# Decay mask moved into a matmul, per-head subtraction in one instruction, state scaling moved to GpSimd, and one set of row exponentials made a group earlier

## The reference, cut to what matters

```python
a_cs = jnp.cumsum((dt * a)...)                       # decay exponents, summed inside a chunk
seg = a_cs[..., :, None] - a_cs[..., None, :]        # row exponent minus column exponent
decay = jnp.exp(jnp.where(causal, seg, -jnp.inf))    # masked: zero above the diagonal
cb = jnp.einsum('bclgn,bcsgn->bcgls', cm, bm)
y_diag = jnp.einsum('bcgls,bcgjls,bcsgjp->bclgjp', cb, decay, xdt)
def step(s, inp):
    dec, st = inp
    return dec[..., None, None] * s + st, s          # the state from chunk to chunk
y_off = jnp.einsum('bclgn,bcgjpn,bcgjl->bclgjp', cm, s_prev, jnp.exp(a_cs))
```

## Time and profile before

| | |
|---|---|
| median of 3 runs | 1851.03 us |
| profiled execution, its own time | 1850.61 us |
| its span | 1849.0 us |
| TensorE busy / VectorE / ScalarE / GpSimd | 88% / 39% / 22% / 14% of the span |
| mean granted TensorE clock | 0.957 of full |
| the SSD groups, from the first group's last x transposes | 134.05 us to 692.44 us of the span |

### The profile page before, as it was taken

One profiled execution on the slowest core, in us unless ns is written; L12 is line 12 of the kernel. 1 busy time (PEld: TensorE's weight loads), 2 busy tenths in 40 slices (PEclk: granted clock), 3 DMA queues, 4 the chain that ended last, 5 costly groups with the idle time before them and its releaser, 6 DMA issues. The chain is left out here.

```text
span 1849.0 us, 23337 instructions
## 1 busy us (share of the span) xinstructions
PE 1635.9 (88%) x9042; PEld 872.5 (47%) x9043; DVE 729.7 (39%) x1304; ACT 413.0 (22%) x769; POOL 264.6 (14%) x287
## 2 busy tenths in 40 slices
PE   4998798799789769999999999999999958999893
PEld 2554454354445334544545545444656434555451
DVE  2545644664654564700016766214025122222124
ACT  4332323233233232000013332410110111111112
POOL 0004402412330440000000000000000012222122
PEclk9998999899899989999999999999989969999997
DMA  9710101011021016712111100214340656998994
GB/s 348 293 46 1 46 23 46 32 37 46 1 91 46 1 49 244 253 46 93 46 46 45 46 18 28 91 46 153 138 181 1 227 224 231 393 343 290 393 385 155
DMA packets 106755, 241.24 MB, mean 130 GB/s; under 512 B 5481, under 2 KB 15214, under 8 KB 106690
## 3 DMA queue, kind: packets, MB, share of 16 engines
q1 hardware_dynamic: 86800, 180.60, 27.1%
q0 software_dynamic: 14288, 48.96, 7.4%
q10 hardware_dynamic: 5602, 10.78, 1.6%
HBM read 218.31 MB, written 22.02 MB: 130 GB/s over the span
## 5 line engine op out<-in xcount | busy, mean ns | idle before, releaser
L439 PE MATMUL psum<-arena 128*128 128x512 f32 x688 | 302.8, 596 | 10.6 <-ACT arena L1279 4.4
L439 PEld LDWEIGHTS psum<-arena 128*128 128x128 f32 x688 | 128.6, 190 | 168.2 <-issue 160.9
L1075 PE MATMUL psum<-arena 128*32 128x256 f32 x2816 | 165.5, 387 | 1.6 <-DVE arena L2193 1.5
L453 PE MATMUL psum<-arena 128*128 128x512 f32 x352 | 155.4, 601 | 1.6 <-issue 1.6
L627 PE MATMUL psum<-arena 128*128 128x512 f32 x256 | 124.9, 626 | 1.0 <-ACT arena L1319 1.0
L1075 PEld LDWEIGHTS psum<-arena 128*32 128x32 f32 x2816 | 91.9, 111 | 60.0 <-issue 7.0
L764 PE MATMUL psum<-arena 128*128 128x512 f32 x256 | 111.5, 593 | 0.0
L453 PEld LDWEIGHTS psum<-arena 128*128 128x128 f32 x352 | 67.3, 193 | 84.0 <-issue 83.7
L2301 POOL TENSOR_TENSOR arena<-arena 128x512 f32<-128x512 f32 x64 | 84.2, 1327 | 131.9 <-ACT arena L1374 131.9
L1729 DVE SCALAR_TENSOR_TENSOR arena<-arena 128x772 f32<-128x772 f32 (+1 forms) x96 | 93.9, 978 | 3.4
L2271 POOL TENSOR_TENSOR arena<-arena 128x512 f32<-128x512 f32 x40 | 46.5, 1174 | 336.1 <-ACT arena L1319 282.1
(11 more groups left out here) (363 smaller groups left out, 2122.8 us busy)
## 6 DMA issues: line engine op xcount, KB each, us to landing
arena<-exp_w_d SPq DMA_DIRECT2D x48, 2048.0 KB, 17.3
arena<-w_in_d SPq DMA_DIRECT2D x22, 2048.0 KB, 7.9
arena<-ada_w_d POOLq DMA_DIRECT2D x8, 2048.0 KB, 9.3
slots<-arena POOLq DMA_DIRECT2D x1, 9216.0 KB, 27.1
arena<-ada_w_d SPq DMA_DIRECT2D x4, 2048.0 KB, 21.5
arena<-ssd_proj_d SPq DMA_DIRECT2D x4, 2048.0 KB, 9.8
slots<-arena POOLq DMA_DIRECT2D x92, 64.0 KB, 4.9
arena<-slots POOLq DMA_DIRECT2D x22, 256.0 KB, 6.0
```

What stands on the lines that cost most here:

```text
L439: ins = mmul(ps[:, 0:T], slot[:, k, m * P:(m + 1) * P], src[:, k, C:NT], start=(k == 0), stop=(k == KD - 1))
L453: ins = mmul(ps[:, 0:n], src[:, k, t * P:(t + 1) * P], slot[:, k, 0:n], start=(k == 0), stop=(k == KD - 1))
L1075: ins = mmul(psU[q * R:(q + 1) * R, 0:2 * HF], XT[:, k % 2, k // 2, :], w13[p][:, :, k, q * HF:(q + 1) * HF], start=(k == 0), stop=(k == K ...
```

## The change

- `rows_of` gets a second matmul, `identb` times `shut[d]`, added into the same bank. `shut[d]` is a bf16 square, 0 where the mask is 1 and -1e30 where it is 0. It lies in memory of `tmpd[0]` and is made once.
- `exponents` is one `tensor_tensor` over 512 columns without the clamp. `cb` is one unmasked copy, and GpSimd multiplies both directions by it.
- GpSimd scales the states (`scale_state`) into a new tile `Send`; VectorE waits for it and adds kv.
- E of direction 0 of group g+1 is made during the direction-1 decays of group g (`spread(g + 1, 0, b)` after each pair). Group 0 makes its own as before.
- `Z_FRONT` is 10 and not 11, two steps of z stand ahead of `first_state`, and the middle one of `Z_STATES` is 2 and not 3.
- `add_square` comes after all `finish` calls of a group. Two small constants (`d_col`, the epsilon) are made at the start.

```diff
-        Z_FRONT = 11
-        Z_STATES = (3, 3, 3, 2, 2)
+        Z_FRONT = 10
+        Z_STATES = (3, 3, 2, 2, 2)
...
                     pe.wait_ge(*is_free(("acsT", d)))
-                    ins = mmul(ps[:, :], selb[0:3 * SH, hh:hh + 1].to_broadcast([3 * SH, P]),
-                               rowsT[0:3 * SH, d, :], start=True, stop=True)
+                    mmul(ps[:, :], selb[0:3 * SH, hh:hh + 1].to_broadcast([3 * SH, P]),
+                         rowsT[0:3 * SH, d, :], start=True, stop=False)
+                    ins = mmul(ps[:, :].rearrange("p (c l) -> p c l", c=TL), identb,
+                               shut[d].unsqueeze(1).to_broadcast([P, TL, P]), start=False, stop=True)
...
+                z_part(2)
                 first_state(0, 4, 8)
                 for i in range(2, 6):
                     for b in range(2):
-                        spread((i - 2) // 2, (i - 2) % 2 * 2 + b)
+                        if g == 0 or i >= 4:
+                            spread(g, (i - 2) // 2, (i - 2) % 2 * 2 + b)
...
                             for i in range(2 * b + 2, min(2 * b + 4, 7)):
                                 next_part(g + 1, i)
+                            if g < SG - 1:
+                                spread(g + 1, 0, b)
... ScalarE
                         run(mm[n % NM], mm[n % NM], ACT.Exp).then_inc(S_("decay_ready"), 1)
+                        if d and g < SG - 1 and h in (3, 5, 7):
+                            spread_out(g + 1, 0, (h - 3) // 2)
                     if d == 0:
                         z_silu(3)
+                if g < SG - 1:
+                    spread_out(g + 1, 0, 3)
... VectorE
-                            step(v.tensor_tensor(heads(vtmp), heads(S[(i - 1) % 2]), per_head(eend), ALU.mult))
-                            ins = v.tensor_tensor(S[i % 2], vtmp, bank(key)[:, :], ALU.add)
+                            dve.wait_ge(S_("S_scaled"), (g * 2 + d) * 3 + i - 1)
+                            ins = v.tensor_tensor(S[i % 2], Send, bank(key)[:, :], ALU.add)
...
-                    for c in range(TL):
-                        ins = v.tensor_scalar(mm[n % NM][:, c, :], bank(key)[:, c * P:(c + 1) * P],
-                                              acs[:, TC + c, at:at + 1], 0.0, ALU.subtract, ALU.min)
-                    ins.then_inc(is_free(key)[0], 1)
+                    v.tensor_tensor(mm[n % NM], bank(key)[:, :].rearrange("p (c l) -> p c l", c=TL),
+                                    acs[:, TC:TT, at:at + 1].to_broadcast([P, TL, P]), ALU.subtract).then_inc(is_free(key)[0], 1)
...
-                    if b:
-                        add_square(g, b - 1)
...
                 finish(2)
                 finish(3)
+                for b in range(3):
+                    add_square(g, b)
... GpSimd
+                def scale_state(d, i):
+                    pool.wait_ge(*is_free(("kv", g, d, i - 1)))
+                    hs = d * SH + g * HPG
+                    g_.tensor_tensor(heads(Send), heads(S[(i - 1) % 2]),
+                                     eend[:, ORDER[d][i], hs:hs + HPG].unsqueeze(2).to_broadcast([P, HPG, SHD]),
+                                     ALU.mult).then_inc(S_("S_scaled"), 1)
...
                 for i in range(2, 5):
                     make_xw(0, i)
+                    scale_state(0, i)
...
-                        g_.tensor_tensor(mm[n % NM], mm[n % NM], cb[d], ALU.mult).then_inc(S_("M_ready"), 1)
+                        g_.tensor_tensor(mm[n % NM], mm[n % NM], cb, ALU.mult).then_inc(S_("M_ready"), 1)
                         if d == 0 and h in (1, 2, 4):
                             make_xw(1, 2 + h // 2)
+                        if d == 0 and h in (1, 3, 4):
+                            scale_state(1, 2 + h // 2)
```

More of the change, by code:

```diff
@@ L175, in build @@
         cb_mem = top[0]
-        cb = [alloc(TL, P) for _ in range(2)]
+        cb = alloc(TL, P)
         NM = 4
@@ L179, in build @@
         S = [alloc(GW) for _ in range(2)]
+        Send = alloc(GW)
         assert top[0] - cb_mem >= KD * 512 and tok_mem + KD * 512 <= top[0]
@@ L192, in build @@
         d_col = small[:, 0:SI // P]
+        shut = [tmpd[0].rearrange("p t h -> p (t h)")[:, 0:P].bitcast(BF16)[:, d * P:(d + 1) * P] for d in range(2)]
         assert RAW % 2 == 0
@@ L641, in rows_of, with spread @@
                     pe.wait_ge(*is_free(("acsT", d)))
-                    ins = mmul(ps[:, :], selb[0:3 * SH, hh:hh + 1].to_broadcast([3 * SH, P]),
-                               rowsT[0:3 * SH, d, :], start=True, stop=True)
+                    mmul(ps[:, :], selb[0:3 * SH, hh:hh + 1].to_broadcast([3 * SH, P]),
+                         rowsT[0:3 * SH, d, :], start=True, stop=False)
+                    ins = mmul(ps[:, :].rearrange("p (c l) -> p c l", c=TL), identb,
+                               shut[d].unsqueeze(1).to_broadcast([P, TL, P]), start=False, stop=True)
                     ins.then_inc(is_full(key)[0], 1)
-                def spread(d, b):
+                def spread(g, d, b):
                     key = ("E", g, d, b)
@@ L1321, in xtok_evac @@
                     blk = g * 4 + m
-                    if blk == 0:
-                        act.wait_ge(S_("d_cols"), 1)
                     run(yT[:, blk, :], yT[:, blk, :], ACT.Identity, scale=d_col[:, blk:blk + 1], bias=0.0)\
@@ L1361, in _, with spread_out @@
                 xtok_evac(3)
-                for d in range(2):
+                def spread_out(g, d, b):
+                    key = ("E", g, d, b)
+                    act.wait_ge(*is_full(key))
+                    run(E[d][:, b, :], bank(key)[:, :], ACT.Exp).then_inc(is_free(key)[0], 1)
+                if g == 0:
                     for b in range(HPG // 2):
-                        key = ("E", g, d, b)
-                        act.wait_ge(*is_full(key))
-                        run(E[d][:, b, :], bank(key)[:, :], ACT.Exp).then_inc(is_free(key)[0], 1)
+                        spread_out(0, 0, b)
                 for d in range(2):
@@ L1369, in _ @@
                         z_silu(1)
+                        for b in range(HPG // 2):
+                            spread_out(g, 1, b)
                         z_silu(2)
@@ L1391, in _ @@
             act.wait_ge(*is_full(("rrow",)))
-            act.wait_ge(S_("eps_set"), 1)
             run(rrow, bank(("rrow",))[:, :], ACT.Sqrt, scale=1.0 / SI, bias=small[:, 62:63]).then_inc(is_free(("rrow",))[0], 1)
@@ L1680, in _ @@
                     .then_inc(S_("hT_ready"), 1)
+            dve.wait_ge(S_("rows_in"), 16)
+            step(v.memset(small[:, 62:63], EPS))
+            step(v.tensor_copy(d_col[0:SHD, :], r_("ssd_d")[0:SHD, 0::2]))
+            step(v.tensor_copy(d_col[SHD:P, :], r_("ssd_d")[SHD:P, 1::2]))
             for i in range(2):
@@ L1689, in _ @@
             dve.wait_ge(S_("rows_in"), 16)
-            v.tensor_copy(d_col[0:SHD, :], r_("ssd_d")[0:SHD, 0::2])
-            v.tensor_copy(d_col[SHD:P, :], r_("ssd_d")[SHD:P, 1::2]).then_inc(S_("d_cols"), 1)
             dve.wait_ge(*is_full(("dt",)))
@@ L1747, in _ @@
             dve.wait_ge(S_("consts_in"), 16 * 2)
+            for d in range(2):
+                v.tensor_scalar(shut[d], mask[d], -1.0, 1e30, ALU.add, ALU.mult)
             step(v.tensor_copy(identb, ident))
@@ L1790, in _ @@
                     dve.wait_ge(S_("M_ready"), g * 2 * HPG)
[L1791 to L1795, removed]
-                ins.then_inc(is_free(key)[0], 1)
+                v.tensor_copy(cb, bank(key)[:, :].rearrange("p (c l) -> p c l", c=TL)).then_inc(is_free(key)[0], 1)
                 conv(g, "x", 2)
@@ L1882, in _ @@
                 finish(3)
+                for b in range(3):
+                    add_square(g, b)
             add_square(SG - 1, 3)
             dve.sem_inc(S_("ssum_ready"), 1)
-            v.memset(small[:, 62:63], EPS).then_inc(S_("eps_set"), 1)
             for s in range(4, 12):
```

## The result

| | before | after |
|---|---|---|
| median (runs) | 1851.78 us (4) | 1810.12 us (4; 1807.78 to 1811.38) |
| ratio, 95% interval | | 0.9774 (0.976 to 0.9788) |
| profiled execution, its own time | 1850.61 us | 1807.78 us |
| its span | 1849.0 us | 1806.2 us |
| VectorE / GpSimd busy in the span | 729.7 / 264.6 us | 665.0 / 282.8 us |

The forecast was 1814 us. The time lies 4 us from it and well inside the range. The sum behind it was less exact than that: -36.8 us were forecast, and the two profiled executions differ by 42.8. A, D0 and D1 gained 11.3 us more than forecast; the second group's projections and the code ahead of the first A lost 5.7 us that the forecast did not have. That these partly hide each other is luck: without those 5.7 us the time would lie 9 to 10 us from the forecast and not 4. And experiment 1 shows that one term (A) was right for a reason that is half wrong.

A forecast was written before the change was run, and what follows sets the result against it. TensorE, busy 88% of the span, was taken as the bound: its work, waits and clock. Terms -28.1 - 11.2 + 5.2 - 2.7 = -36.8 us took 1850.61 to 1813.8, stated as 1814 us, range 1798 to 1836.

The forecast's parts named there:

- A: Stretch from the last x transposes to the first rows (states of direction 0): 23.3 us, -28.1 us over four groups.
- D0: Stretch from the first rows to the last product of direction 0: 31.9 us a group, -11.2 us over four groups.
- D1: Rest of the group after direction 0's last product: +1.6 us in three groups, +0.4 in the last, +5.2 in all.
- (a): In A: transposes 0.89 us sooner, two z steps fill 1.78 of 2.27 us waiting for xw; 0.5 us stays.
- (b): In A: early E removes the 2.68 us wait ahead of the second off in groups 1 to 3; group 0 keeps 0.6.
- (c): In A: GpSimd's scaling (1.04 us, up to 1.49) is hidden; xdt queued behind costs the fourth state about 0.3 us.
- rival 1: Shorter waits keep the clock at 2.4 GHz, in D0 and behind each last pair: 11.6 us, giving 1802; chance 0.15.
- rival 2: Mask matmuls at 0.38 us add 10, L1816 at 1.62 in three steps of each A another 4: 1828; chance 0.22.
- The last wait of D0: Ahead of direction 0's last pair: 5.4 us left of the 6.76 us chain, of which TensorE still waits 4.5.
- Group ends: Moving add_square finishes y and the B and C copies 1.3 us earlier, cutting two TensorE waits: -2.7 us.
- Rival 3: In D0, direction 1's scalings queue behind products on GpSimd: 10.1 us a group, 40.6 in all, 1854; chance 0.07.
- Rival 4: Waits only move: A gives about 14 us, the masks take 14, so 1850, no change; chance 0.06.

The follow-up runs named there:

- experiment 1: Changed kernel with the early E undone, every group making its own E of direction 0: 1808.63 us, ratio 0.9758.
- Experiment 3: Changed kernel with the subtraction as four instructions again, with the clamp, mask matmul kept: 1821.49 us, ratio 0.9835.
- experiment 10: Changed kernel with add_square between the finish calls again: 1817.41 us, ratio 0.98.
- experiment 6: Changed kernel with ScalarE's squares of y's first three blocks ahead of the Exp of the next group's last E: 1805.12 us, ratio 0.9753.
- experiment 5: Changed kernel with VectorE's subtraction for direction 0's head 7 ahead of direction 1's last state step: 1786.86 us, ratio 0.9658.

## Why the prediction was right, point by point

- **Stretch A: right in sum, the reason half wrong.** 23.3 us was forecast, 22.74 measured; (a) left a wait of 0.4 us (forecast 0.5), and the first group's wait ahead of the second off is 0.56 (forecast 0.6). Point (b) gave the gain at the second off in groups 1 to 3 to the early E. The first group, which has no early E, should have told me otherwise: by my own sum its wait fell from 2.7 to 0.6 through the scaling alone. Experiment 1 shows that the same holds in every group. What the early E saves in A (2.3 us a group) it costs in D1 and in ScalarE's order. (c) was too careful: no step of A waits for xdt. The terms written down add up to 23.0 us and not 23.3; without the 0.3 of (c) they give 22.7, which is what was measured.
- **Stretch D0: the step that was mis-sized.** The walk head by head gave pairs at 8.4, 15.0, 22.4 and 30.75 us; they came at 8.3, 15.0, 21.9 and 30.18. I then left a low clock of 1.2 us a group in. It was not there: the clock of the four D0 was 1.00, 0.97, 1.00 and 0.97, and the 0.97 cost nothing, as all four took 30.18 us. So of the 6.9 us that D0 gained beyond the forecast 4.6 are the clock and 2.3 the walk. The *old* D0 had a clock of 0.84 to 0.90. This is the first half of rival 1, and it held; the second half (full clock behind the last pair) did not, as the wait there stayed. Experiment 3 has 1.5 to 1.6 us for a fall of the clock in D0, in three groups of four.
- **The mask matmuls: right.** 0.22 us each in place. Doubled they cost 0.09 each on the average (0.16 to 0.18 in D0, less in D1), and rival 2 (0.38 each) falls. Its other 4 us do not follow from its own terms either: an addition of 1.62 and not 0.69 us is 0.93 more, within the slack of 1.1.
- **The rule against GpSimd, and the port.** Each scaling took 1.04 us, 1.5 times VectorE's 0.69, in line with the row the forecast used and less than the "about twice" of the Trainium skill ("GPSIMD Engine Reference", "Engine selection"). What counts is that it stands beside off and L1827. VectorE's additions to y, which were to meet GpSimd more often, met it less: the median of 32 was 0.72 us and the longest 1.81, against 1.37 and 1.68 before.
- **The last wait of D0: right.** 5.38 us of chain, 4.33 of wait, low clock behind it. (By the rows of before TensorE works 6.76 - 5.70 = 1.06 us of the chain, so the forecast's own 5.4 gives 4.3 and not 4.5.)
- **D1: too dear.** The last pair came 21.7 us after D1's first row, as walked (21.75). The stretch as a whole grew by less than forecast in the first and third group (+0.6 and +0.4, clock 0.94 against 0.90 before) and by more in the second (+2.4, 0.91 against 0.94). In the last group it fell by 1.7, of which 1.3 are the wait for `finish` (2.1 to 0.8), as forecast.
- **Group ends: one step failed.** "Y is finished 1.3 us earlier after the last pair, and so are ScalarE's copies of B and C": the first half holds (experiment 10). The second does not, because the last of the new Exps stands in ScalarE's queue ahead of all four squares. Before, the squares of y's first two blocks were taken ahead of the last pair; now all four wait for TensorE's last spread, which starts 0.9 us behind that pair, and the copy comes 6.4 us behind the pair and not 5.1. So the wait grew by 1.3 us where I had it shrink by 1.3. I had moved the four spreads past TensorE's and ScalarE's bank waits, but not past ScalarE's squares. Experiments 1 and 6 both undo it, to 3.3 and 3.9 us.
- **Rival 3** (scalings behind products) did not come: the scaling is nowhere named as what TensorE or VectorE waited for, and no scaling took more than 1.05 us. **Rival 4** did not come either: A, counted as in the table, gained 30.1 us and not 14. Its 1850 also leaves out what the forecast had for D0 and D1.

## What to carry to other kernels

When two engines form a loop, list for each wait the chain behind it, instruction by instruction, in each engine's written order, and ask of every member whether it has to be in the chain: the largest gain of one edit here (experiment 5: 23 us by the median, 19 in the stretches of its profile) was an instruction that had its data and stood behind one that had not. A wait that is cut from 4.3 to 1.3 us gives more than its own length if the clock stays up; and a producer that is moved into an earlier stage (the early E) has to be followed through every queue it now stands in, not only the one it left.

## What the runs showed of the hardware that was not expected

- The same code falls to the low clock in one execution and not in another. D0 of the changed kernel is 30.18 us in four groups of one profile; in the profile of experiment 6, which leaves D0 alone, the first group's took 31.83 at a clock of 0.94, with the same waits. The matmuls right behind the second of two waits, 0.87 and 0.88 us, already run slow (L684 in 1.98 us; behind the same two waits it took 1.10 in the changed kernel's profile):

```profile
161.80 1.13 PE L677 MATMUL psum<-arena 128*128 128x128 f32 x8 [0.87 <-DVE arena L1836]
163.81 1.98 PE L684 MATMUL psum<-arena 128*128 128x512 f32 x2 [0.88 <-DVE arena L1827]
165.72 1.84 PE L717 MATMUL psum<-arena 128*64 128x128 f32 x16
167.49 1.99 PE L629 MATMUL psum<-arena 128*128 128x512 f32 x4
```

  So a single profile can differ by 1.6 us a group. Outside the groups it is more. The first A starts at 131.6 to 136.8 us in ten profiles of kernels in which TensorE does the same up to there; the clock was 0.99 in the shortest and 0.95 in the longest. What follows the last group took 1149.9 to 1157.9 us in the fourteen profiles (experiment 5 has the shortest). The table's +2.1 us before the first A is within that. What decides it stays open.
- What single parts cost when undone (scaling 9 us, subtraction 11, z 8, squares 7, early E -1) does not add up to the gain of 42: it is some 35, and the mask matmuls' 5.5 would have to come off. Scaling and mask part show it directly: undone together they cost 25 us, one by one 9 + 11 - 5.5, which is 15.
